# Attention output as values by transposed weights, with the softmax division moved to GpSimd ahead of it

## The chip, the cores and the metric

The kernel runs on one core of one Trainium2 chip. The metric is the device time of one execution in microseconds. Three runs of the kernel before took 2192.15, 2194.88 and 2196.93 us, so its median is 2194.88 us.

## The reference

The program is a trunk of two layers (`DEPTH = 2`) over 512 tokens of width 1024. Each layer is a SwiGLU half-step, a mixer with three groups of heads, and a second SwiGLU half-step. The change touches two of the three groups:

```
# group A: 6 heads x 64, each of 4 blocks of 128 queries, keys 0 .. end of the block,
#          128 keys chosen per query by an indexer, bias by distance
logits = q @ k.T / 8 + bias (+ -inf for keys not chosen or not admissible)
p      = softmax(logits, axis=-1)
out_a  = p @ v                       # 128 queries x 64, per head
# group C: 4 heads x 64, every query over 256 memory tokens
p      = softmax(q @ k_mem.T / 8, axis=-1)
out_c  = p @ v_mem
x      = x + concat(out_a, out_b, out_c) @ w_out
```

A softmax is exp(logit - maximum) divided by the row's sum. The division can be done on the weights (128 x keys) or on the output (128 x 64), with the same result but for rounding.

## The kernel before

**Engines and queues.** Each engine runs its own program in order. The order of work in the mixer is written out by hand in one list, `MIX_ORDER` (L197 to L363), which every engine walks through, doing its own share of each step and waiting on semaphores for the others. All large products are done in three passes over rounded halves (XH, XL of the activations, wh, wl of the weights; lines 886, 887, 888, the helper `three`). Weights come in units of 1 MB: SP loads `raw`, ScalarE (or, for units 16 and 17 of the mixer, GpSimd in `round_weights`, L851) makes `wh`, VectorE makes `wl` (`split_lo_rows`, L1724).

**Attention.** A job is one head for one block of 128 queries. Two jobs with neighbouring heads form a pair, and 20 pairs make a layer's attention: pairs 0 to 7 are memory jobs (256 keys), 8 to 10 are block 0 of group A (128 keys), 11 to 13 block 1 (256 keys), 14 to 16 block 2 (384), 17 to 19 block 3 (512). They go through a pipeline of 24 slots, `("att", slot)` in `MIX_ORDER`. In slot s the engines do:

- TensorE, in this order (`attention`, L1265): if a phase (a block of one group) ended with pair s-4, transposes of the divided output `oA` (L1271); transposes of the weights `at` of pair s-2 (L1285), after `je_done`; the logits of pair s (L1301), two heads in the two row halves of the array; the output of pair s-3 (L1317), with the transposed weights `pT` (128 x 128) as the stationary operand and the values (128 x 64) as the moving one, one 128 x 64 output per head in bank 3.
- VectorE (`attention`, L1988): the low half `XL` of a finished phase (L1995); the reciprocals `rrec` of all sums of a phase at its end (L2003); the row maxima of pair s (L2022 with bias, L2026 without); at the end of a phase the output times the reciprocals into `oA` (L2033).
- ScalarE (L1602): exp of pair s-1 with the row sum (L1616); the high half `XH` of a finished phase (L1623); copies of the transposed weights of pair s-2 from PSUM to `pT` (L1634).
- GpSimd (`combine`, L832): the sum of bias strip and mask for pair s+2, from pair 11 on, so in slots 9 to 17 (L848).

**What fills the gaps.** Between the slots `MIX_ORDER` puts rounds of the output projection on TensorE (`out_round`, L1035, one round is the three instructions of lines 886 to 888 with 512 columns): 3, 3, 2, 3, 3, 2, 3, 3, 2, 2 of them after slots 3 to 12, then 1, 1, 1, 2, 1, 1, 1, 2, 1, 1 after slots 13 to 22. On VectorE there are a selection round in slots 5 to 12 (L1830, L1832), the additions of finished rounds into `xT` (L2063) and pieces of `wl` (L1734). After slot 22 the rest of the projection follows in one piece (`TAIL`).

Of the kernel before, what the change touches and what calls it, by code (L numbers as in the profile page):

```python
# [14 lines left out]
P = 128  # L15
# [492 lines left out]
jl_done jm_done je_done jtr_done jp_even jp_odd jv_done  # L508
o_ev o_t o_hi o_lo
# [3 lines left out]
def hybrid_trunk(nc, xt, memt, cols, strip_table, weights, consts, out):  # L513
    depth = cols.shape[1]

    with ExitStack() as ctx:
# [119 lines left out]
        oA = sb("oA", [P, WA])  # L636
# [41 lines left out]
        with nc.Block() as block:  # L678
# [56 lines left out]
            def _(pool):  # L735
                def layer(L):
# [94 lines left out]

                    def combine(p):  # L832

                        for n in (2 * p, 2 * p + 1):
                            if n >= N_JOBS:
                                return
                            b, j = job(n)
                            if b and j < H_A:
                                m = masked_count(b, j)
                                w = P * (b + 1)  # L840
                                if m == 1:
                                    pool.wait_ge(S["strip_in"], 48)
                                    pool.wait_ge(S["jv_done"], M_JOBS)
                                if j == 0:
                                    pool.wait_ge(S["unsel_done"], b)
                                if m > 4:
                                    pool.wait_ge(S["jm_done"], n - 3)
                                pool.tensor_tensor(comb[(m - 1) % 4][:, 0:w], strips[j][:, T - w:], unsel[b][:, :],  # L848
                                                   ALU.add).then_inc(S["cb_done"], 1)
# [8 lines left out]
                    for step in MIX_ORDER:  # L858
                        if step[0] == "att":
                            combine(step[1] + 2)  # L860
# [13 lines left out]
            def _(pe):  # L874
                def layer(L):
# [389 lines left out]
                    def attention(slot):  # L1265
                        p = slot - 4
                        if 0 <= p < N_PAIRS and phase_end(p):
                            b, ph, done = phase(2 * p)
                            pe.wait_ge(S["o_ev"], done + 1)
                            for c in range(3 if ph else 2):  # L1270
                                mm = pe.transpose(bank[3][:, c * P:(c + 1) * P], oA[:, c * P:(c + 1) * P],  # L1271
                                                  const("ident"))
                            mm.then_inc(S["o_t"], 1)
                        p = slot - 2
                        if 0 <= p < N_PAIRS:
                            for e in range(2):
# [4 lines left out]
                                pe.wait_ge(S["je_done"], n + 1)  # L1281
# [22 lines left out]
                        if 0 <= p < N_PAIRS:  # L1304
                            for e in range(2):
                                n = 2 * p + e
                                b, j = job(n)
                                pe.wait_ge(S["jp_odd" if e else "jp_even"], p + 1)
                                if n == 0:
                                    pe.wait_ge(S["os_read"], of("os_read", NB))  # L1310
                                if j in (0, H_A) and n:
                                    pe.wait_ge(S["o_lo"], phase(n)[2])
                                nt = b + 1 if j < H_A else 2
                                at0 = DH * (j if j < H_A else j - H_A)
                                for i in range(nt):
                                    v = (dvN[:, i, at0:at0 + DH] if j < H_A else mvN[:, i, at0:at0 + DH])
                                    mm = pe.matmul(bank[3][:, at0:at0 + DH], pT[n % 4][:, i * P:(i + 1) * P], v,  # L1317
                                                   start=(i == 0), stop=(i == nt - 1))
                                mm.then_inc(S["jv_done"], 1)
# [30 lines left out]
            def _(act):  # L1350
# [21 lines left out]
                def layer(L):  # L1372
# [229 lines left out]
                    def attention(slot):  # L1602
# [16 lines left out]
                        if 0 <= p < N_PAIRS and phase_end(p):  # L1619
                            b, ph, done = phase(2 * p)  # L1620
                            act.wait_ge(S["o_t"], done + 1)
# [60 lines left out]
            def _(dve):  # L1682
# [27 lines left out]
                def layer(L):  # L1710
# [277 lines left out]
                    def attention(slot):  # L1988
# [8 lines left out]
                        p = slot - 3  # L1997
                        ends = 0 <= p < N_PAIRS and phase_end(p)
                        if ends:
                            b, ph, done = phase(2 * p)  # L2000
                            j0, nh = (0, H_A) if ph else (H_A, H_M)
                            dve.wait_ge(S["je_done"], 2 * p + 2)
                            chain.step(dve.reciprocal(rrec[:, b % 2, j0:j0 + nh], rsum[:, b % 2, j0:j0 + nh]))  # L2003
                            chain.join()
# [22 lines left out]
                        if ends:  # L2027
                            p = slot - 3
                            b, ph, done = phase(2 * p)
                            j0, nh = (0, H_A) if ph else (H_A, H_M)  # L2030
                            dve.wait_ge(S["jv_done"], 2 * p + 2)
                            r = rrec[:, b % 2, j0:j0 + nh].unsqueeze(2).to_broadcast([P, nh, DH])
                            dve.tensor_tensor(oA[:, 0:nh * DH].rearrange("p (h d) -> p h d", h=nh),  # L2033
                                              bank[3][:, 0:nh * DH].rearrange("p (h d) -> p h d", h=nh), r,
                                              ALU.mult).then_inc(S["o_ev"], 1)
# [135 lines left out]
```

## Time and profile before

| | us |
|---|---|
| median of 3 runs | 2194.88 |
| lowest and highest run | 2192.15, 2196.93 |
| span of the profiled execution, first to last instruction | 2192.3 |
| TensorE busy | 2169.3 (99%) |
| VectorE busy | 1076.5 (49%) |
| ScalarE busy | 765.7 (35%) |
| GpSimd busy | 383.4 (17%) |

The span is what the profile shows of the execution's own time; the profile states no other time for it, and the three timed runs lie from 0.2 us below to 4.6 us above it. A fp32 product or a fp32 weight load stands in the trace as two records, a transpose or a rounded (fp32r) product as one. In the timelines the first column is the start in us from the start of the span, the second the length of the merged piece; the ends of TensorE's records are modelled, so what an instruction costs TensorE is read here from its start to the start of the next.

### The profile page before, as it was taken

The page shows a single profiled execution, that of the slowest core. Times are in us where ns is not written, and L with a number is a line of the kernel's source. Part 1 is how long each engine was busy: PE and PEld are TensorE (multiplying, and loading weights), DVE is VectorE, ACT ScalarE, POOL GpSimd, SP SyncE. Part 2 cuts the span into 40 slices and gives each one's busy share as a digit, 9 for nine tenths or more (in the row PEclk, how much of TensorE's full clock was granted, in tenths as well). Part 3 has the DMA queues.
Part 4 walks back from the last instruction along what each step waited for, and adds up shares of the span by engine and source line. Part 5 has one row for each costly group of instructions (what it writes and reads, how often), then busy time and mean ns, then how long its engine had stood idle before and what let it go on. Part 6 is the DMA issues. An engine that isn't in the chain of part 4 may idle for free.

```text
span 2192.3 us, 32889 instructions
## 1 busy us (share of the span) xinstructions
PE 2169.3 (99%) x13657; PEld 1755.9 (80%) x13657; DVE 1076.5 (49%) x1473; ACT 765.7 (35%) x1038; POOL 383.4 (17%) x319
## 2 busy tenths in 40 slices
PE   9999999999999999999999999999999999999999
PEld 7888888777777888888888888887777778888887
DVE  5333333788657544333343433338877666333322
ACT  5222223474335332222232222234733454222211
POOL 0111012005223410101111110130151134111000
PEclk9999999999999999999999999999999999999999
DMA  5222233221011222223222222232211112322232
GB/s 190 96 96 96 89 105 114 97 97 31 32 68 39 78 96 96 96 91 106 93 96 97 96 100 99 89 125 86 97 41 39 51 39 80 112 96 96 91 105 73
DMA packets 30649, 192.40 MB, mean 88 GB/s; under 512 B 3216, under 2 KB 5392, under 8 KB 11984
## 3 DMA queue, kind: packets, MB, share of 16 engines
q1 hardware_dynamic: 30160, 189.80, 25.4%
q8 instruction: 81, 1.33, 0.2%
q10 hardware_dynamic: 384, 1.07, 0.1%
q14 instruction: 24, 0.20, 0.0%
HBM read 188.64 MB, written 2.10 MB: 87 GB/s over the span
## 4 chain that ended last, share of the span: by engine, by line
PE 91%; DVE 5%; ACT 2%; issue 1%; DMA 0%; SPq 0%; DVEq 0%; ACTq 0%
PE psum L886 27%; PE psum L888 26%; PE psum L887 26%; PE psum L1317 2%; PE psum L1169 1%; PE psum L1017 1%; PE psum L1301 1%; PE psum L1189 1%; PE psum L1285 1%; DVE acc L1817 1%; PE psum L1259 1%; PE psum L1227 1%; DVE XL L1749 1%; PE psum L1221 1%; DVE wl L1734 1%
## 5 line engine op out<-in xcount | busy, mean ns | idle before, releaser
L886 PE MATMUL psum<-XH,wh 128*128 128x512 f32 x1904 | 763.4, 401 | 4.9 <-DVE wl L1734 1.8
L888 PE MATMUL psum<-XH,wl 128*128 128x512 f32 x1904 | 743.8, 391 | 0.0
L887 PE MATMUL psum<-XL,wh 128*128 128x512 f32 x1904 | 743.7, 391 | 0.0
L886 PEld LDWEIGHTS psum<-XH,wh 128*128 128x128 f32 x1904 | 358.6, 188 | 93.2 <-issue 14.6
L888 PEld LDWEIGHTS psum<-XH,wl 128*128 128x128 f32 x1904 | 358.6, 188 | 76.0
L887 PEld LDWEIGHTS psum<-XL,wh 128*128 128x128 f32 x1904 | 358.8, 188 | 74.1 <-issue 4.3
L1742 DVE TENSOR_TENSOR wl<-raw,wh 128x2048 fp32r<-128x2048 f32 x88 | 201.7, 2292 | 159.4 <-ACT wh L1387 159.4
L886 PE MATMUL psum<-HH,wh 128*128 128x512 f32 x704 | 273.9, 389 | 0.0
L887 PE MATMUL psum<-HL,wh 128*128 128x512 f32 x704 | 273.9, 389 | 0.0
L888 PE MATMUL psum<-HH,wl 128*128 128x512 f32 x704 | 273.9, 389 | 0.0
L1382 ACT ACTIVATE wh<-raw 128x2048 fp32r<-128x2048 f32 (+1 forms) x84 | 157.2, 1872 | 307.6 <-PE psum L888 307.4
L750 POOL TENSOR_TENSOR sg<-sg,rF 128x512 f32<-128x512 f32 x88 | 113.5, 1292 | 783.5 <-ACT sg L1412 783.5
L1720 DVE TENSOR_TENSOR wl<-raw,wh 128x2048 fp32r<-128x2048 f32 x52 | 122.1, 2347 | 251.4 <-ACT wh L1382 251.3
L1387 ACT ACTIVATE wh<-raw 128x2048 fp32r<-128x2048 f32 x88 | 167.4, 1902 | 13.1 <-PE psum L888 13.1
L1418 ACT ACTIVATE HH<-hf 128x512 f32 (+1 forms) x88 | 55.6, 632 | 328.3 <-DVE hf L1771 328.3
L1412 ACT ACTIVATE sg<-sg 128x512 f32<-128x512 f32 x88 | 55.2, 631 | 292.9 <-DVE sg L1763 292.9
L1763 DVE TENSOR_TENSOR sg<-psum,rF 128x512 f32<-128x512 f32 x88 | 60.1, 687 | 193.5 <-PE psum L888 172.2
L886 PEld LDWEIGHTS psum<-HH,wh 128*128 128x128 f32 x704 | 132.1, 188 | 27.6
L887 PEld LDWEIGHTS psum<-HL,wh 128*128 128x128 f32 x704 | 132.1, 188 | 27.6
L888 PEld LDWEIGHTS psum<-HH,wl 128*128 128x128 f32 x704 | 132.1, 188 | 27.1
L1771 DVE TENSOR_TENSOR hf<-sg,psum 128x512 f32<-128x512 f32 x88 | 60.4, 687 | 134.2 <-PE psum L888 125.8
L672 POOL TENSOR_TENSOR sg<-xT 128x512 f32<-128x512 f32 x40 | 47.8, 1196 | 395.9 <-DVE xT L1786 333.4
(255 smaller groups left out, 2123.1 us busy)
## 6 DMA issues: line engine op xcount, KB each, us to landing
raw<-weights SPq DMA_DIRECT2D x143, 1024.0 KB, 4.9
raw<-weights SPq DMA_DIRECT2D x32, 896.0 KB, 4.6
xT<-xt SPq DMA_DIRECT2D x4, 512.0 KB, 6.4
memT<-memt SPq DMA_DIRECT2D x2, 1024.0 KB, 4.7
out<-xT SPq DMA_DIRECT2D x8, 256.0 KB, 5.6
stripsA<-strip_table SPq DMA_DIRECT2D x2, 768.0 KB, 6.7
raw<-weights SPq DMA_DIRECT2D x2, 512.0 KB, 6.6
stripsB<-strip_table SPq DMA_DIRECT2D x2, 512.0 KB, 7.3
```

Of the source, the lines that this page charges most:

```text
L750: pool.tensor_tensor(sg[fs][:, :], sg[fs][:, :], rF[:, :], ALU.mult).then_inc(S["gr_done"], 1)
L886: pe.matmul(out_ap, a_hi, b_hi, start=first, stop=False)
L887: pe.matmul(out_ap, a_hi, b_lo, start=False, stop=False)
L888: return pe.matmul(out_ap, a_lo, b_hi, start=False, stop=last)
L1382: ins = act.activation(wh[u % 2][:, k0:k1, :], raw[u % 2][:, k0:k1, :], ACT.Copy)
L1387: act.activation(wh[j][:, :, :], raw[j][:, :, :], ACT.Copy).then_inc(S["w_hi"], 1)
L1412: act.activation(sg[fs][:, :], sg[fs][:, :], ACT.Silu).then_inc(S["gs_done"], 1)
L1418: act.activation(HH[:, 2 * i + fs, :], hf[fs][:, :], ACT.Copy).then_inc(S["hh_done"], 1)
L1720: dve.tensor_tensor(wl[u % 2][:, :, :], raw[u % 2][:, :, :], wh[u % 2][:, :, :].bitcast(F32), ALU.subtract).then_inc(S["w_lo"], 1)
L1742: dve.tensor_tensor(wl[j][:, :, :], raw[j][:, :, :], wh[j][:, :, :].bitcast(F32), ALU.subtract).then_inc(S["w_lo"], 1)
L1763: dve.tensor_tensor(sg[fs][:, :], bank[fs][:, :], rF[:, :], ALU.mult).then_inc(S["g_free"], 1)
L1771: dve.tensor_tensor(hf[fs][:, :], sg[fs][:, :], bank[2 + fs][:, :], ALU.mult).then_inc(S["u_free"], 1)
```

## The change

The two heads of a pair now put their values (128 x 64) in as stationary operands, one in each column half of the array, and the transposed weights (128 queries wide) stream through. The output comes out as 2 x 64 rows by 128 queries, which is the form that the projection wants, so `oA`, its multiplication and the transposes of it go. The division by the sum can then no longer be applied to the output's partitions, so it is done on the weights before they are transposed: VectorE takes the reciprocals pair by pair, in slot s for pair s-1 after the maxima of pair s, and GpSimd multiplies each job's weights by them in `normalise`, in slot s for pair s-1 ahead of `combine`. TensorE's transposes wait for that (`jn_done`) instead of for the exp.

```diff
+                    def normalise(p):
+                        if 0 <= p < N_PAIRS:
+                            pool.wait_ge(S["jr_done"], p + 1)
+                            for n in (2 * p, 2 * p + 1):
+                                b, j = job(n)
+                                w = P * (b + 1) if j < H_A else NM
+                                pool.tensor_scalar(at[n % 4][:, 0:w], at[n % 4][:, 0:w], rrec[:, b % 2, j:j + 1], None,
+                                                   ALU.mult).then_inc(S["jn_done"], 1)
...
                         if step[0] == "att":
+                            normalise(step[1] - 1)
                             combine(step[1] + 2)
...  TensorE, attention(slot)
-                            pe.wait_ge(S["o_ev"], done + 1)
-                            for c in range(3 if ph else 2):
-                                mm = pe.transpose(bank[3][:, c * P:(c + 1) * P], oA[:, c * P:(c + 1) * P],
-                                                  const("ident"))
-                            mm.then_inc(S["o_t"], 1)
...
-                                pe.wait_ge(S["je_done"], n + 1)
+                                pe.wait_ge(S["jn_done"], n + 1)
...
-                                for i in range(nt):
-                                    v = (dvN[:, i, at0:at0 + DH] if j < H_A else mvN[:, i, at0:at0 + DH])
-                                    mm = pe.matmul(bank[3][:, at0:at0 + DH], pT[n % 4][:, i * P:(i + 1) * P], v,
+                            for i in range(nt):
+                                for e, r in enumerate(rows):
+                                    mm = pe.matmul(bank[3][r, at0:at0 + P],
+                                                   vals[:, i, at0 + DH * e:at0 + DH * (e + 1)],
+                                                   pT[(2 * p + e) % 4][:, i * P:(i + 1) * P],
                                                    start=(i == 0), stop=(i == nt - 1))
...  ScalarE
-                            act.wait_ge(S["o_t"], done + 1)
+                            act.wait_ge(S["jv_done"], 2 * p + 2)
...  VectorE, attention(slot)
-                            dve.wait_ge(S["je_done"], 2 * p + 2)
-                            chain.step(dve.reciprocal(rrec[:, b % 2, j0:j0 + nh], rsum[:, b % 2, j0:j0 + nh]))
-                            chain.join()
...
-                            dve.tensor_tensor(oA[:, 0:nh * DH].rearrange("p (h d) -> p h d", h=nh),
-                                              bank[3][:, 0:nh * DH].rearrange("p (h d) -> p h d", h=nh), r,
-                                              ALU.mult).then_inc(S["o_ev"], 1)
+                        p = slot - 1
+                        if 0 <= p < N_PAIRS:
+                            b, j = job(2 * p)
+                            dve.wait_ge(S["je_done"], 2 * p + 2)
+                            dve.reciprocal(rrec[:, b % 2, j:j + 2], rsum[:, b % 2, j:j + 2]).then_inc(S["jr_done"], 1)
```

## Rows read from the trace of the kernel before

**Rows 1.** The page: the chain that ended last, share of the span by engine.
```profile
PE 91%; DVE 5%; ACT 2%; issue 1%; DMA 0%; SPq 0%; DVEq 0%; ACTq 0%
```
**Rows 2.** Table by windows, first layer: PE, PEld, DVE, ACT, POOL; clock, DMA.
```profile
638.00:641.00 3.00, 1.44 (x10) 0.70 (x8) 2.11 (x4) 3.00 (x12) 3.00 (x4) 0.93 0.00 0
641.00:644.00 3.00, 2.91 (x13) 2.26 (x13) 3.00 (x5) 1.53 (x6) 0.53 (x1) 0.50 0.00 0
```
**Rows 3.** Timeline of TensorE, first layer: slots 5, 12, 16 to 17, 19, start of TAIL.
```profile
653.87 0.70 PE L1301 MATMUL psum<-mkT,mqT 64*128 64x256 f32 x4
...
681.06 0.70 PE L1301 MATMUL psum<-dkT,dqT 64*128 64x256 f32 x4
...
694.17 0.92 PE L1301 MATMUL psum<-dkT,dqT 64*128 64x384 f32 x4
695.01 1.10 PE L1317 MATMUL psum<-dvN,pT 128*128 128x64 f32 x8
695.93 0.48 PE L886 MATMUL psum<-XH,wh 128*128 128x512 f32 x1
...
697.72 0.82 PE L1285 MATMUL psum<-cst,at 128*128 128x128 f32 x6
698.47 1.13 PE L1301 MATMUL psum<-dkT,dqT 64*128 64x512 f32 x4
...
706.59 1.13 PE L1301 MATMUL psum<-dkT,dqT 64*128 64x512 f32 x4
...
722.66 0.46 PE L886 MATMUL psum<-XH,wh 128*128 128x512 f32 x1
```
**Rows 4.** Groups by line: the output products and the transposes that go.
```profile
L1317 PE MATMUL psum<-dvN,pT 128*128 128x64 f32 x240 | 31.3, 277 | 1.3 <-DVE XL L1995 1.1
...
L1317 PE MATMUL psum<-mvN,pT 128*128 128x64 f32 x128 | 18.9, 294 | 0.8 <-DVE XL L1995 0.8
...
L1271 PE MATMUL psum<-cst,oA 128*128 128x128 f32 x40 | 7.3, 281 | 1.2 <-DVE oA L2033 1.2
```
**Rows 5.** TensorE's idle time at line 1271, by what ended it: us, times.
```profile
  DVE oA L2033: 4.7, 8
```
**Rows 6.** Timeline of TensorE in the recurrence: one column half; both in turn; one tile.
```profile
588.72 0.56 PE L1235 MATMUL psum<-U,kdc 64*64 64x64 f32 x12
589.12 0.52 PE L1241 MATMUL psum<-AT,U 64*64 64x64 f32 x12
589.47 0.86 PE L1259 MATMUL psum<-gvN,XTF 64*64 64x64 f32 x12
...
593.43 0.87 PE L1221 MATMUL psum<-Sbd,WT 128*64 128x128 f32 x6
594.23 0.88 PE L1227 MATMUL psum<-EGr,Sbd 128*128 128x64 f32 x6
```
**Rows 7.** GpSimd by line and shape: busy us, mean ns of one.
```profile
L855 POOL CAST wh<-raw 128x1024 fp32r<-128x1024 f32 x8 | 8.9, 1156 | 6.7 <-PE psum L888 6.7
L848 POOL TENSOR_TENSOR comb<-stripsA,acc 128x512 f32<-128x512 f32 x6 | 7.6, 1290 | 4.1 <-DVE mxs L2022 4.1
...
L848 POOL TENSOR_TENSOR comb<-stripsA,acc 128x256 f32<-128x256 f32 x6 | 4.3, 740 | 66.8 <-issue 66.8
```
**Rows 8.** Timeline of VectorE: slots 5 to 6 and 18.
```profile
654.60 0.76 DVE L2026 TENSOR_REDUCE mxs<-psum 128x1 f32<-128x256 f32 x2 [0.22 <-PE psum L1301]
655.27 0.68 DVE L1830 MAX8 m<-wrk 128x8 f32<-128x512 f32 x1
...
656.66 0.68 DVE L2063 TENSOR_TENSOR xT<-psum,xT 128x512 f32<-128x512 f32 x1
657.25 0.17 DVE L2003 RECIPROCAL rrec<-rsum 128x4 f32<-128x4 f32 x1
...
703.59 0.69 DVE L2022 CUSTOM_DVE_ANT_0 at<-psum,comb 128x512 f32<-128x512 f32 x1 [2.64 <-PE psum L1301]
...
704.81 1.22 DVE L1734 TENSOR_TENSOR wl<-raw,wh 128x1024 fp32r<-128x1024 f32 x1
```

More of the change, by code:

```diff
@@ L507 @@
 v_t v_done gc_ps gc_ready row_ps row_ready
-jl_done jm_done je_done jtr_done jp_even jp_odd jv_done
-o_ev o_t o_hi o_lo
+jl_done jm_done je_done jr_done jn_done jtr_done jp_even jp_odd jv_done
+o_hi o_lo
 """.split()
@@ L1265, in attention @@
                     def attention(slot):
-                        p = slot - 4
-                        if 0 <= p < N_PAIRS and phase_end(p):
-                            b, ph, done = phase(2 * p)
-                            pe.wait_ge(S["o_ev"], done + 1)
-                            for c in range(3 if ph else 2):
-                                mm = pe.transpose(bank[3][:, c * P:(c + 1) * P], oA[:, c * P:(c + 1) * P],
-                                                  const("ident"))
-                            mm.then_inc(S["o_t"], 1)
                         p = slot - 2
@@ L1304, in attention @@
                         if 0 <= p < N_PAIRS:
[L1305 to L1314, printed above, removed]
-                                for i in range(nt):
-                                    v = (dvN[:, i, at0:at0 + DH] if j < H_A else mvN[:, i, at0:at0 + DH])
-                                    mm = pe.matmul(bank[3][:, at0:at0 + DH], pT[n % 4][:, i * P:(i + 1) * P], v,
+                            b, j = job(2 * p)
+                            pe.wait_ge(S["jp_even"], p + 1)
+                            pe.wait_ge(S["jp_odd"], p + 1)
+                            if p == 0:
+                                pe.wait_ge(S["os_read"], of("os_read", NB))
+                            elif j in (0, H_A):
+                                pe.wait_ge(S["o_lo"], phase(2 * p)[2])
+                            nt = b + 1 if j < H_A else 2
+                            vals, at0 = (dvN, DH * j) if j < H_A else (mvN, DH * (j - H_A))
+                            for i in range(nt):
[3 more added lines that the diff above has]
+                                                   pT[(2 * p + e) % 4][:, i * P:(i + 1) * P],
                                                    start=(i == 0), stop=(i == nt - 1))
-                                mm.then_inc(S["jv_done"], 1)
+                                    if i == nt - 1:
+                                        mm.then_inc(S["jv_done"], 1)
                     if L == 0:
@@ L1996, in attention @@
                                               XH[sl].bitcast(F32), ALU.subtract).then_inc(S["o_lo"], 1)
[L1997 to L2001, printed above, removed]
-                            dve.wait_ge(S["je_done"], 2 * p + 2)
-                            chain.step(dve.reciprocal(rrec[:, b % 2, j0:j0 + nh], rsum[:, b % 2, j0:j0 + nh]))
-                            chain.join()
                         p = slot
@@ L2026, in attention @@
                                     dve.tensor_reduce(m, src, AX.X, ALU.max, negate=True).then_inc(S["jm_done"], 1)
[L2027 to L2032, printed above, removed]
-                            dve.tensor_tensor(oA[:, 0:nh * DH].rearrange("p (h d) -> p h d", h=nh),
-                                              bank[3][:, 0:nh * DH].rearrange("p (h d) -> p h d", h=nh), r,
-                                              ALU.mult).then_inc(S["o_ev"], 1)
+                        p = slot - 1
+                        if 0 <= p < N_PAIRS:
+                            b, j = job(2 * p)
+                            dve.wait_ge(S["je_done"], 2 * p + 2)
+                            dve.reciprocal(rrec[:, b % 2, j:j + 2], rsum[:, b % 2, j:j + 2]).then_inc(S["jr_done"], 1)
                     ffn(0)
```

1 line of the change is left out of this document (removed).

## The prediction

> **What bounds the kernel now.** I read the chain of waits first. TensorE carries 91% of it [rows 1], and the table in the section above has it busy for 2169.3 of 2192.3 us, so a TensorE instruction that goes pays its full time, as long as TensorE does not then meet a wait. All of the change lies in the attention stage, which in the first layer runs from about 632 to 722.66 us and again in the second. There the timeline of TensorE shows the slots as a fixed sequence [rows 3]: transposes, logits, output products, rounds. The logits of slots 5, 12 and 19 start at 653.87, 681.06 and 706.59, with lengths on TensorE of 0.64, 0.64 and 1.06 (L in the list below), so they end at 654.5, 681.7 and 707.65: 27.2 us for seven slots, then 25.9 us for seven. Those three ends and 722.66 are my marks. The table by windows is the third view: the one low-clock stretch of the stage, 0.50 at 641 to 644, comes right after three microseconds in which TensorE was busy for 1.44 [rows 2].
>
> The pieces of a slot, read from start to next start [rows 3, 8]:
> - T, the transposes of a pair at 384 keys: 697.72 to 698.47, 0.75; by six transposes against two, four and eight, 0.31, 0.53 and 0.97 for 128, 256 and 512 keys.
> - L, the logits at 384 keys: 694.17 to 695.01, 0.84, and by 0.21 less or more for each 128 keys: 0.42, 0.64, 1.06.
> - R, a round: 695.93 to 697.72 holds two and three of the transposes that go (0.11 each): 0.73, and I use 0.70.
> - M, both maxima of a pair: 654.60 to 655.27, 0.67 at 256 keys; 703.59 to 704.81, 1.22 at 512; 0.95 between, 0.42 at 128. A reciprocal is 0.17; a selection round 655.27 to 656.66, 1.4; an addition into xT 0.6; a half of `wl` 1.1 to 1.2.
> - A wait passed from one engine to the next costs about 0.1: the step from the end of the logits to the maxima is 0.1.
>
> **The change part by part.**
>
> *Output products.* Before, 368 records are busy for 31.3 + 18.9 = 50.2 us [rows 4]; from start to next start eight of them (a pair at 256 keys) take 695.01 to 695.93, 0.92 [rows 3], so 0.46 per 128 keys of a pair, 0.115 a record. After, there are as many records, each a load of 64 columns and a stream of 128. The nearest row is L1221, the very form, six records in one column half: 593.43 to 594.23, 0.133 each [rows 6]. If the two halves of the array work one after the other, this is the price and 0.07 per 128 keys is lost (upper bound, 0.53). Whether they work at once, the neighbouring rows tell: L1235 feeds the column halves in turn and starts 12 records in 0.40 us, 0.033 each; L1259 has all 12 in one tile and lasts 0.86, 0.07 each. So halves in turn run twice as fast. I take half of 0.133, which is also twice L1235's 0.033 for a stream twice as wide: V = 0.27, 0.53, 0.80, 1.07 us for 128, 256, 384, 512 keys, against 0.46, 0.92, 1.38, 1.84. The lower bound is L1235's 0.033 itself, half of that.
>
> The trace shows a gap ahead of narrow tiles (it is inside the 0.133). The Trainium skill (TensorEngine Tiling (Array Packing), Key Properties) says that changing the tiling mode drains TensorE, which speaks against this change: each pair gets one switch more, from the row halves of the logits to column halves and on to the whole array. By the page the switch would be paid whole instead of half, an estimate of 0.1 us more a pair, so some 2 us more where TensorE is the bound; the sum goes by the rows.
>
> *The end of a phase.* 40 transposes go (L1271, 0.11 each, 4.4 us), and with them TensorE's wait for `oA`, 4.7 us in 8 places [rows 5]. VectorE loses 16 multiplications and gets 24 reciprocals more, about even.
>
> *The new link.* For pair q-1 the weights are now ready only after: logits of q end, 0.1, M(q), reciprocal 0.17, 0.1, two normalisations 2N, 0.1. Then come T(q-1) and L(q+1), and only then the next link can begin. Behind the waiting transposes on TensorE stand those logits, and behind them all of the slot; behind the reciprocal on VectorE stand selection, additions and `wl`; behind `normalise` on GpSimd stand `combine` and, in slots 1 to 4, the casts of units 16 and 17. What covers the link on TensorE is V(q-3) and the rounds, from 0.27 + 1.4 to 0.53 + 2.1 early, but only V + 0.7 from slot 13 on.
>
> *N.* No row shows GpSimd with one tensor input and a column of scalars. Bounds: the cast, 1024 elements in 1.156 us, which is 1.1 ns an element with one input; the sum of two tensors, 0.74, 1.0, 1.29 for 256, 384, 512 [rows 7]. The rows of sums make 2.15 ns an element and 0.19 fixed; with this fixed part in the cast, 0.86 to 0.95 an element are left. I take N = 0.29, 0.40, 0.51, 0.62 us for 128, 256, 384, 512 keys, since the operation has one tensor input as the cast has. The lower end is the cast without a fixed part, 0.14 to 0.58, the upper the row of sums.
>
> The skill (GPSIMD Engine Reference, Elementwise — side-by-side cycle accounting) gives 769 ns measured for 512 elements of a tight one-input loop. The cast here is faster than that. With an estimate of N = 0.77 at 512 from that page the total below would be some 3 us higher.
>
> *Slots 0 to 5.* Slot 2 is held at 637.7 by the copy of the last values as before. Transposes of pair 1 wait for maxima that VectorE takes at 638.8, a reciprocal and 0.8 of GpSimd, until 640.6; the logits behind them begin at about 641.2 instead of 641.09. The casts of units 16 and 17 move from 637 to 641.5 apart, to 637.6, 640.6, 645 and 650; VectorE asks for them at 640.6, 644, 649 and after 660, so only their order changes. In slots 3 and 4 the shorter V brings about 1, and `oA` no longer stands before `wl` of unit 17, for which TensorE waits near 651: 0.5. Logits of slot 5 end at 653.0 instead of 654.5: -1.5.
>
> *Slots 5 to 12.* Period = max(V + R, link) + T + L, with VectorE not later than its own work. Slot 5: V + R 1.93, link 0.1 + 0.67 + 0.17 + 0.1 + 0.8 + 0.1 = 1.94, with T and L 3.12 (before 3.54). The same sum gives for slots 6 to 11: 3.80, 3.58, 3.05, 3.38, 3.70, 2.72, where VectorE is late by 0.5 in slot 8, and in slot 10 `combine` of pair 11, which waits for the last memory outputs, keeps normalise 0.1 too long. Sum 23.35 against 27.2: -3.85.
>
> *Slots 12 to 19.* Slot 12 has the last selection round (2.7 us) on VectorE, so maxima 13 start 0.5 late. Periods by the link: 3.30, 3.9, 3.63, 4.07, 4.28, 4.54, 4.98 = 28.7 against 25.9: +2.75. An example, slot 16: 0.1 + 0.95 + 0.17 + 0.1 + 1.02 + 0.1 + 0.75 + 1.06 = 4.25. TensorE alone would need 0.53 + 1.4 + 0.75 + 1.06 = 3.7 there, 2.8 in slot 15, 3.5 in slot 18: it now waits 0.5 to 1.5 a slot. GpSimd has 2N + 2.55 of `combine` = 3.6 in the fullest slot and is not the bound.
>
> *Slots 20 on.* T of pair 18 waits until 2.95 after the last logits (1.5 of it covered), then T 0.97, V 1.07, two rounds 1.4, T 0.97, V 1.07, R 0.7, V 1.07, R 0.7, and the two last rounds 1.4 cover the copies of the output: 12.3 against 15.01: -2.7.
>
> Sum: -1.5 - 3.85 + 2.75 - 2.7 = -5.3 a layer, -10.6 in both. On the profiled execution 2192.3 - 10.6 = 2181.7. The span is 2.6 below the median of the runs shown; with what lies around it unchanged, 2194.9 - 10.6 = 2184.3.
>
> **The rivals.**
>
> *GpSimd is slow: slower than before.* One mechanism: N at the rate of the two-tensor row. For: it is the only arithmetic of GpSimd in the trace. Against: the cast. Each link from slot 12 on gets 0.68, 0.68, 0.98 three times, 1.34, 1.35 longer, 7.0 a layer; the slots with two rounds lose 0.7 three or four times, 2.5; slots 0 to 4 0.5. +20 in all: 2204. It turns to slower where the sum of both normalisations of a 512 pair passes about 2.0 us.
>
> *The gain is eaten.* N midway (0.95 at 512), or the column halves taking turns: V then is 0.53 per 128 keys; the early slots and the end of the stage give back 6.5 to 7 a layer, the late ones nothing, since the link covers it. 2193 to 2198. For: the one row of this form shows no gain. Against: L1235.
>
> *The clock.* Waiting 15 to 40% of each late slot, TensorE falls to its lower level (0.50 is 1.2 GHz), as it did after 638 to 641. T, L, V and R double in seven slots and become the bound at 5 to 7.5 us each: about 14 a layer, 2212. Against: there it was busy less than half of three us, here 60 to 85%.
>
> *It doesn't do what it says*, the products staying as long, is in the second rival. *Better than forecast*: N without fixed part (0.1 to 0.3 a link from slot 12 on, 1.5 a layer) and V half as long (0.27 in eight pairs early and at the end, 2): 2177.
>
> **How the numbers follow.** About 0.2% (4.4 us) is what a measurement of this kernel can tell from no change. The forecast 0.50, with 2184.3 as its time and 2179 to 2190 as its range, better 0.08; the gain eaten 0.20; GpSimd slow 0.15; the clock 0.05; the rest, 0.02, with the slow ones. Faster: 0.50 + 0.08 and a little of the eaten cases, 0.60; same 0.19; slower 0.21. The range leaves out the clock and the worst of GpSimd: 2176 to 2203.
>
> **What would show it.** In the new profile: the output products start at 0.065 to 0.07 a record (0.13 would be the turn-taking halves); `tensor_scalar` on GpSimd at 0.6 for 512 keys (1.3 is the slow rival); TensorE idle before its transposes with GpSimd's normalise as releaser, some 9 us a layer, nearly all after slot 12; logits of slot 5, 12 and 19 earlier by 1.5, 5.4 and 2.6 us than before in the first layer; no low clock but near 641. The prediction is wrong if the waits before the transposes are also there in slots 5 to 11, or if VectorE's reciprocal comes late because it waits behind selection or `wl`.

## The result and the profile after

The changed kernel took 2219.78 us (median of 4 runs, 2216.25 to 2223.03) against 2194.51 us (2192.15 to 2196.93) for the kernel before on the same chip: a ratio of 1.0116, 95% interval 1.0102 to 1.0131. It is 25 us slower; the prediction said 10.6 us faster, and the time lies outside its range. The profiled execution has a span of 2220.5 us (before: 2192.3). TensorE has less work than before, but is busy for 2172.5 us, 3.2 more, and idle for 48.0 us instead of 23.0: part of the loss is waiting, and part stands inside records that became longer at a low clock.

The new multiplications by shape, with the output products and the transposes, whole run (columns as in [rows 4]: busy us, mean ns of one, idle time before and its releaser):

```profile
L838 POOL TENSOR_SCALAR at<-at,rrec 128x256 f32<-128x256 f32 x44 | 51.2, 1175 | 31.9 <-DVE rrec L2027 31.9
L1287 PE MATMUL psum<-cst,at 128*128 128x128 f32 x184 | 38.0, 311 | 35.4 <-POOL at L838 35.2
L1318 PE MATMUL psum<-pT,dvN 128*64 128x128 f32 x240 | 22.0, 323 | 0.0
L838 POOL TENSOR_SCALAR at<-at,rrec 128x512 f32<-128x512 f32 x12 | 20.4, 1711 | 10.9 <-DVE rrec L2027 10.9
L838 POOL TENSOR_SCALAR at<-at,rrec 128x384 f32<-128x384 f32 x12 | 14.8, 1243 | 4.2 <-DVE rrec L2027 4.2
L1318 PE MATMUL psum<-pT,mvN 128*64 128x128 f32 x128 | 11.4, 304 | 0.0
L838 POOL TENSOR_SCALAR at<-at,rrec 128x128 f32<-128x128 f32 x12 | 7.1, 603 | 4.5 <-PE psum L1318 3.3 <-DVE rrec L2027 1.3
```

The reader is to see three things. The products are shorter: 22.0 + 11.4 = 33.4 us of records against 31.3 + 18.9 [rows 4]. TensorE idles 35.4 us ahead of the transposes of the weights, 35.2 of them for line 838 (18.8 us in 24 waits in the first layer, where the prediction had some 9 a layer), and its weight loads wait longer still (52.2 us in the whole run). And one multiplication of 512 keys takes 1.71 us, beyond even the 1.29 of the sum of two tensors [rows 7].

The timeline of TensorE, first layer, at the prediction's four marks (columns as in [rows 3]; in brackets the idle time ahead and its releaser):

```profile
655.37 0.70 PE L1303 MATMUL psum<-mkT,mqT 64*128 64x256 f32 x4
656.00 0.66 PE L1318 MATMUL psum<-pT,mvN 128*64 128x128 f32 x8
656.59 0.50 PE L896 MATMUL psum<-XH,wh 128*128 128x512 f32 x1
...
682.31 0.70 PE L1303 MATMUL psum<-dkT,dqT 64*128 64x256 f32 x4
682.94 0.44 PE L1318 MATMUL psum<-pT,dvN 128*64 128x128 f32 x4
...
707.01 0.88 PE L1318 MATMUL psum<-pT,dvN 128*64 128x128 f32 x12
707.82 0.50 PE L896 MATMUL psum<-XH,wh 128*128 128x512 f32 x1
...
716.75 1.11 PE L1287 MATMUL psum<-cst,at 128*128 128x128 f32 x4 [2.32 <-POOL at L838]
718.28 1.11 PE L1287 MATMUL psum<-cst,at 128*128 128x128 f32 x4 [0.43 <-POOL at L838]
719.33 2.08 PE L1303 MATMUL psum<-dkT,dqT 64*128 64x512 f32 x4
721.34 1.55 PE L1318 MATMUL psum<-pT,dvN 128*64 128x128 f32 x12
...
730.15 1.09 PE L1318 MATMUL psum<-pT,dvN 128*64 128x128 f32 x16
731.18 0.50 PE L896 MATMUL psum<-XH,wh 128*128 128x512 f32 x1
...
735.30 0.40 PE L896 MATMUL psum<-XH,wh 128*128 128x512 f32 x1
```

The logits of slots 5, 12 and 19 end at 656.0, 682.9 and 721.3 (before: 654.5, 681.7, 707.65), and the tail starts at 735.3 (722.66). From mark to mark, in us of one layer:

| stretch | before | forecast | after | after minus forecast |
|---|---|---|---|---|
| to the end of slot 5's logits | 654.5 | 653.0 | 656.0 | +3.0 |
| slots 5 to 12 | 27.2 | 23.35 | 26.9 | +3.6 |
| slots 12 to 19 | 25.95 | 28.7 | 38.4 | +9.7 |
| slot 19 to the tail | 15.0 | 12.3 | 14.0 | +1.7 |

The last column sums to 18.0 us: the first layer is 12.6 us slower than before where the sum had it 5.3 faster (rounding aside). The span grew by 28.2 us, which leaves 15.6 for the second layer, so it went the same way and lost 3 us more. Twice 18.0 and these 3 are the whole error of 38.8 us in the span (2181.7 forecast, 2220.5 measured).

Now GpSimd and VectorE beside each other, five links of the first layer (two timelines, GpSimd first):

```profile
640.83 3.23 POOL L838 TENSOR_SCALAR at<-at,rrec 128x256 f32<-128x256 f32 x2 [1.16 <-DVE rrec L2027]
...
660.92 1.83 POOL L838 TENSOR_SCALAR at<-at,rrec 128x256 f32<-128x256 f32 x2 [2.08 <-DVE rrec L2027]
664.85 2.72 POOL L838 TENSOR_SCALAR at<-at,rrec 128x256 f32<-128x256 f32 x2 [2.10 <-DVE rrec L2027]
...
714.24 3.99 POOL L838 TENSOR_SCALAR at<-at,rrec 128x512 f32<-128x512 f32 x2 [0.71 <-DVE rrec L2027]
722.92 3.10 POOL L838 TENSOR_SCALAR at<-at,rrec 128x512 f32<-128x512 f32 x2 [4.69 <-DVE rrec L2027]
```
```profile
640.65 0.67 DVE L1989 TENSOR_TENSOR XL<-gzT,XH 128x512 fp32r<-128x512 f32 x1
641.24 1.22 DVE L1738 TENSOR_TENSOR wl<-raw,wh 128x1024 fp32r<-128x1024 f32 x1
...
660.75 0.67 DVE L1834 MAX8 m<-wrk 128x8 f32<-128x512 f32 x1
...
662.12 0.68 DVE L2055 TENSOR_TENSOR xT<-psum,xT 128x512 f32<-128x512 f32 x1
...
664.68 1.20 DVE L1738 TENSOR_TENSOR wl<-raw,wh 128x1024 fp32r<-128x1024 f32 x1
...
714.06 1.20 DVE L1738 TENSOR_TENSOR wl<-raw,wh 128x1024 fp32r<-128x1024 f32 x1
```

The pair at 660.92, beside selection and an addition that reads PSUM, takes 1.83, 0.92 a head. The pair at 664.85, beside 1.2 us of `wl`, takes 2.72: 0.9 more. With `wl` and XL beside it, at 640.83, 1.4 more; at 714.24, 0.9 more than the pair at 722.92. `wl` itself stays at 1.2 us, so it is GpSimd that gives way, and the 0.9 us are about what was left of `wl` when GpSimd started (664.85, with `wl` running from 664.68 to the next start at 665.80). It is no chance meeting: the reciprocal releases GpSimd, and the piece of `wl` stands right behind the reciprocal in VectorE's list. In the Trainium skill, the table in GPSIMD Engine Reference, Specifications, says that GpSimd shares its SBUF interfaces with VectorE and contends with instructions of two SBUF inputs; the trace agrees, `wl` and XL having two and the addition at 662.12 one.

The table by windows (PE, PEld, DVE, ACT, POOL; clock, DMA): three windows of the late slots of the first layer, and from the same view one that holds those of the second:

```profile
700.00:715.00 15.00, 11.27 (x71) 6.14 (x71) 6.50 (x19) 8.28 (x20) 13.37 (x12) 1.00 0.00 0
715.00:719.00 4.00, 1.83 (x8) 1.42 (x8) 0.86 (x2) 0.60 (x2) 3.23 (x2) 0.72 0.63 207
719.00:723.00 4.00, 4.00 (x19) 1.84 (x18) 1.39 (x5) 1.43 (x4) 0.08 (x1) 0.50 0.13 55
...
1776.00:1813.00 37.00, 31.43 (x160) 17.43 (x158) 19.78 (x61) 18.21 (x53) 29.60 (x31) 0.86 0.00 1
```

Behind the wait of 2.32 us the granted clock is 0.50, which is 1.2 GHz, for the transposes, the logits and the output products of slot 19. The second transposes and the logits stand in the chain: 1.05 and 2.01 us from start to next start instead of 0.58 (726.08 to 726.66) and 1.06, so 1.4 us. The products take 1.47 instead of 0.81, but the next transposes wait for GpSimd behind them in any case. (A low stretch after slot 2 is in both kernels: 0.56 from 640 to 645 before, 0.65 from 645 to 650 after.) In the second layer the clock falls more often: 0.86 in the mean over 37 us, where the same slots of the first layer stood at 1.00 up to 715. The logits of slot 15 in both layers:

```profile
695.63 0.92 PE L1303 MATMUL psum<-dkT,dqT 64*128 64x384 f32 x4
...
1798.53 1.65 PE L1303 MATMUL psum<-dkT,dqT 64*128 64x384 f32 x4
...
1840.41 0.40 PE L896 MATMUL psum<-XH,wh 128*128 128x512 f32 x1
```

The last line is the start of the second tail. From the end of slot 12's logits to the tail the second layer takes 55.8 us (1784.62 to 1840.41), the first 52.4 (682.94 to 735.30), while in the kernel before this stretch has the same length in both layers (41.0). GpSimd's multiplications in it are as long in both layers to 0.01 us a pair. So these 3.4 us are the low clock, and but for 0.4 that come back elsewhere they are the 3 us that the second layer lost more. The clock fell there behind a wait of 1.73 us, ahead of the transposes at 1791.61. The same wait is in the first layer (1.74 ahead of 689.95), where the clock stayed at 2.4 GHz; why, no run shows.

### The profile page after: what moved, and what is told of

It reads as the page before. It is cut to its first block and busy times, and to the rows that moved or that the text cites. A ratio compares the mean times of both kernels' runs of the same rounds, so it can differ in the third digit from the quotient of the medians.

```text
span 2220.5 us, 32911 instructions
## 1 busy us (share of the span) xinstructions
PE 2172.5 (98%) x13617; PEld 1734.2 (78%) x13617; DVE 1068.7 (48%) x1481; ACT 769.0 (35%) x1038; POOL 473.3 (21%) x399
## 3 DMA queue, kind: packets, MB, share of 16 engines
q10 hardware_dynamic: 384, 1.07, 0.1%
## 5 line engine op out<-in xcount | busy, mean ns | idle before, releaser
L897 PEld LDWEIGHTS psum<-HL,wh 128*128 128x128 f32 x704 | 132.2, 188 | 27.2
```

The lines of the kernel that those rows point to most:

```text
L897: pe.matmul(out_ap, a_hi, b_lo, start=False, stop=False)
```

## The experiments

Each edit is against the changed kernel, but for the one that says otherwise. Each was timed beside the kernel before, and the ratio is to that; the medians of the kernel before beside them were 2194.7, 2192.2 and 2195.4 us, so a difference of under 3 us between two experiments means nothing by itself.

**No division: the change without its link.** GpSimd's multiplication is left out and the transposes wait for the exponential, so the weights stay undivided.

```diff
-                            normalise(step[1] - 1)
...
-                                pe.wait_ge(S["jn_done"], n + 1)
+                                pe.wait_ge(S["je_done"], n + 1)
```

> The changed kernel without the division of the weights (GpSimd's normalise left out, the output stays undivided; transposes wait for the exp as before). Theory (the new link through GpSimd is the loss, the output products themselves gain): 2170 to 2182 us, the output products at 0.59 us a pair of 256 keys from start to start, no idle time of TensorE ahead of its transposes, clock at its upper level as before. Rival (the products in column halves, with one more change of tiling a pair, are the loss): 2200 us or more, since they are unchanged here.

Measured: 2170.56 us, ratio 0.9898 (0.988 to 0.9916). As expected, at the lower edge. The logits of slots 12 and 19 start at:

```profile
675.41 0.70 PE L1302 MATMUL psum<-dkT,dqT 64*128 64x256 f32 x4
...
698.46 1.13 PE L1302 MATMUL psum<-dkT,dqT 64*128 64x512 f32 x4
```

Slots 12 to 19 take 23.5 us (from 676.04 to 699.52, the ends of the logits) instead of 38.4. The products and the end of the phases are worth 24 us; the link costs 49.

**The link alone, on the kernel before.** The old products, `oA` and its transposes stay, with `normalise`, its reciprocals and the new wait added, so the output is divided twice.

```diff
+                            normalise(step[1] - 1)
...
-                                pe.wait_ge(S["je_done"], n + 1)
+                                pe.wait_ge(S["jn_done"], n + 1)
```

> The kernel before with the link alone: reciprocals pair by pair behind the maxima, weights multiplied on GpSimd, transposes of the weights wait for it. The output products stay in the old form, the output is multiplied by the reciprocals again and transposed as before (so the division is done twice, which makes the output another one). Theory (the link costs more than the rest of the change gains, above all in slots 12 to 19, where it sets the period whatever the products take): slots 12 to 19 at 36 to 39 us as in the change, 2222 to 2238 us. Rival (link and products only lose together, for instance by the changes of tiling): 2200 to 2210 us.

Measured: 2232.02 us, ratio 1.0172 (1.0143 to 1.0201), and slots 12 to 19 in 36.7 us. As expected. Alone the link costs 37.5 us (39.8 against the kernel before timed beside it, 2192.2), with the shorter products 49: these no longer cover it. From here the products bring back only 12 to 15 us (2232.0 to 2219.8, or by the two differences to the kernel before) of the 24 that they are worth without it.

**VectorE multiplies, behind the reciprocal.**

```diff
-                            normalise(step[1] - 1)
...  VectorE, behind the reciprocal of the pair
+                                dve.tensor_scalar(at[n % 4][:, 0:w], at[n % 4][:, 0:w], rrec[:, b % 2, j:j + 1], None,
+                                                  ALU.mult).then_inc(S["jn_done"], 1)
```

> The changed kernel with the same multiplication of the weights on VectorE, right behind its reciprocal, instead of on GpSimd. Theory (GpSimd's slow tensor_scalar is the price, 0.92 to 1.7 us each; a VectorE tensor_scalar over 512 elements took 0.43 us in the selection): link shorter by 1.3 to 2.5 us a slot, 2180 to 2192 us. Rival A (any division ahead of the transposes costs about this, since the wait for the maxima of the next pair is what matters): 2205 us or more. Rival B (VectorE becomes the bound in slots 5 to 12, where selection runs): faster than the change, but slots 5 to 12 longer than before the change.

Measured: 2201.49 us, ratio 1.0035 (1.0023 to 1.0046). A miss, by 10 us. The timeline of VectorE shows the same line 2031 at very different lengths, with GpSimd's `combine` beside the second and third (the second fence):

```profile
643.62 0.62 DVE L2031 TENSOR_SCALAR at<-at,rrec 128x256 f32<-128x256 f32 x2
...
692.09 1.66 DVE L2031 TENSOR_SCALAR at<-at,rrec 128x256 f32<-128x256 f32 x2
...
696.76 2.38 DVE L2031 TENSOR_SCALAR at<-at,rrec 128x384 f32<-128x384 f32 x2
```
```profile
692.54 1.06 POOL L857 TENSOR_TENSOR comb<-stripsC,acc 128x384 f32<-128x384 f32 x1
...
696.31 2.62 POOL L857 TENSOR_TENSOR comb<-stripsA,acc 128x512 f32<-128x512 f32 x2 [2.72 <-DVE mxs L2017]
```

Alone it needs 0.31 a head at 256 keys, beside `combine` 0.83, and the pair of 384 ends only when `combine` does. Here it is VectorE that gives way, and I had left that out. In both kinds of meeting the instruction that started second is the one that became longer: `wl` had started ahead of GpSimd's multiplication above, `combine` (691.58, 696.31) ahead of VectorE's here. The short multiplication saves 18 us of the changed kernel's time; that this stretching is what keeps it from more is argued from these lines, no run takes it away. The rival in which VectorE's selection becomes the bound is out: slots 5 to 12 take 25.95 us here (653.87 to 679.82), less than the 26.9 of the change and the 27.2 of before.

**The reciprocal ahead of the maxima.** The five lines of the reciprocal move from behind the maxima of pair s to the front of slot s in VectorE's list; GpSimd multiplies as in the change.

```diff
+                            dve.reciprocal(rrec[:, b % 2, j:j + 2], rsum[:, b % 2, j:j + 2]).then_inc(S["jr_done"], 1)
                             (row maxima of pair s)
-                            dve.reciprocal(rrec[:, b % 2, j:j + 2], rsum[:, b % 2, j:j + 2]).then_inc(S["jr_done"], 1)
```

> The changed kernel with VectorE's reciprocal of pair s-1 ahead of the maxima of pair s instead of behind them; GpSimd multiplies as in the change. Theory (the loss is a loop logits, maxima, reciprocal, GpSimd, transposes, next logits inside one slot; its place in the order matters as much as GpSimd's speed): the multiplication no longer stands behind the maxima of the next pair, what is left is GpSimd's own load of about 5 us in slots 15 to 17: 2180 to 2195 us. Rival (only the time of GpSimd's instructions matters, and it meets other work anyway): within 8 us of the change, 2212 to 2222.

Measured: 2194.12 us, ratio 0.9996 (0.9986 to 1.0005): as expected, at the upper edge. The logits of q and their maxima leave the link, and 25.7 us come back; the time is that of before. The rival, that only the time of GpSimd's instructions matters, is out.

**Two-tensor form.** The multiplication on GpSimd as `tensor_tensor`, the column of reciprocals spread over the keys.

```diff
-  pool.tensor_scalar(at[n % 4][:, 0:w], at[n % 4][:, 0:w], rrec[:, b % 2, j:j + 1], None,
+  pool.tensor_tensor(at[n % 4][:, 0:w], at[n % 4][:, 0:w],
+                     rrec[:, b % 2, j:j + 1].to_broadcast([P, w]),
```

> The changed kernel with GpSimd's tensor_scalar written as tensor_tensor with the reciprocal's column broadcast along the keys. Theory (the instruction's time is the term that was mis-sized): 0.74, 1.0 and 1.29 us for 256, 384 and 512 keys as the two-tensor rows have it, against 0.92, 1.24 and 1.55 alone, so 0.4 to 0.5 us less a slot, 2204 to 2213 us. Rival (GpSimd's time is not what the slots wait for): same as the change within 3 us.

Measured: 2199.34 us, ratio 1.0028 (1.0018 to 1.0037). A miss, 5 us better than I expected:

```profile
L838 POOL TENSOR_TENSOR at<-at,rrec 128x512 f32<-128x512 f32 x12 | 13.9, 1190 | 7.9 <-DVE rrec L2028 7.9
L838 POOL TENSOR_TENSOR at<-at,rrec 128x384 f32<-128x384 f32 x12 | 9.7, 827 | 4.0 <-DVE rrec L2028 4.0
```

The form with two tensors is the quicker one at every width (0.83 against 1.24 us at 384), and quicker than the sum of two tensors, which takes 1.0 there, between the two of [rows 7]. Same place, same waits, same engine: 20.4 us from the size of N alone.

**The same instruction over half the keys.** GpSimd multiplies the first half of each job's keys; the other half stays undivided.

```diff
-  pool.tensor_scalar(at[n % 4][:, 0:w], at[n % 4][:, 0:w], rrec[:, b % 2, j:j + 1], None,
+  pool.tensor_scalar(at[n % 4][:, 0:w // 2], at[n % 4][:, 0:w // 2], rrec[:, b % 2, j:j + 1], None,
```

> The changed kernel, but GpSimd multiplies only the first half of the keys of each job; the weights of the other half go to the transposes undivided (so they are not softmax weights). Order, waits and instruction counts stay; only the width of the multiplication is halved. My theory (the size of this multiplication was the term that the prediction had wrong; 0.60, 0.93, 1.24 and 1.55 us for 128, 256, 384 and 512 keys when alone in the changed kernel): the multiplication falls by about half, to 0.3, 0.6, 0.76 and 0.92 us alone, close to but still above the 0.29, 0.40, 0.51 and 0.62 us that the prediction took. So 2188 to 2200 us, slots 12 to 19 in 26 to 32 us instead of 38.4. Rival (the place in the order and the wait, not the width, cost the time): 2212 us or more.

Measured: 2199.13 us, ratio 1.0018 (1.0009 to 1.0028); slots 12 to 19 take 711.38 + 1.06 - 679.72 = 32.7. By the median as expected at its edge, by the slots just above it: N means 0.77 for the 192 columns of a 384 pair. The fixed part does not halve:

```profile
L838 POOL TENSOR_SCALAR at<-at,rrec 128x192 f32<-128x192 f32 x6 | 4.5, 766 | 2.1 <-DVE rrec L2027 2.1
L838 POOL TENSOR_SCALAR at<-at,rrec 128x64 f32<-128x64 f32 x6 | 2.6, 447 | 2.5 <-PE psum L1318 1.8 <-DVE rrec L2027 0.6
```

With 0.60, 0.92, 1.24 and 1.55 for 128 to 512 columns that makes one line, 0.29 us fixed and 2.45 ns a column.

**ScalarE multiplies**, as an activation (Copy) with the reciprocals as its scale, last in its share of the slot. Once with the reciprocal ahead of the maxima, and once behind them as in the change.

```diff
-                            normalise(step[1] - 1)
...  ScalarE, end of attention(slot)
+                            act.wait_ge(S["jr_done"], p + 1)
+                            for n in (2 * p, 2 * p + 1):
+                                act.activation(at[n % 4][:, 0:w], at[n % 4][:, 0:w], ACT.Copy,
+                                               scale=rrec[:, b % 2, j:j + 1]).then_inc(S["jn_done"], 1)
```

> The changed kernel with the reciprocal ahead of the maxima and the weights multiplied on ScalarE (Copy with the reciprocal's column as scale) at the end of its slot. Theory (what cost the time is the pair of GpSimd and VectorE getting in each other's way and the loop behind the maxima; ScalarE is busy for half of a slot and is not stretched by either): 0.45 to 0.7 us an instruction, slots 13 to 18 at most 4.1 us each (ScalarE's own sum at 512 keys: exp 1.8, copies 1.1, multiplications 1.3), 2174 to 2184 us. Rival (ScalarE, with 4 us of work in the late slots, becomes the bound and its copies to pT come late): slots 12 to 19 above 30 us, 2190 us or more.

> The multiplication on ScalarE (2174.6 us when the reciprocal stands ahead of the maxima), with the reciprocal back behind the maxima as in the changed kernel: the fourth cell of place against engine (GpSimd behind 2219.8, ahead 2194.1). Theory (the place sets when the factor is there, some 0.5 us later per slot, and ScalarE's queue then holds the exponentials of the next slot back behind the wait): 2182 to 2196 us. Rival (only the engine counts): 2172 to 2178 us.

Measured: 2174.56 us ahead (2172.95 to 2177.41, ratio 0.9915, 0.9886 to 0.9943), and 2195.97 us behind (ratio 1.001, 0.9998 to 1.0021). Both as expected, at the lower and at the upper edge. The first beats both kernels, 17.7 us below the kernel before timed beside it (2192.22) and some 4 us above the kernel with no division. Its group at 256 keys, and TensorE's wait for it in the attention stage of the first layer (us, times, longest):

```profile
L1645 ACT ACTIVATE at<-at,rrec 128x256 f32<-128x256 f32 x44 | 20.0, 506 | 4.5 <-DVE rrec L2012 4.5
```
```profile
PE psum L1286 <- ACT at L1645: 0.8, 1, 0.8
```

That is 0.8 us where the same view of the changed kernel has 18.8. Its weight loads of that line wait some more for ScalarE (4.5 us in the whole run).

**Both mends of GpSimd's link together**: reciprocal ahead, two-tensor form.

> The two edits that each gave about 20 to 25 us together: the reciprocal ahead of the maxima on VectorE, and the multiplication on GpSimd as a two-tensor operation with the reciprocals' column spread over the keys. Theory (place and size of the link both count, and what is left once the link is short is GpSimd's own load): 2183 to 2190 us. Rival (GpSimd's load alone bounds it in either form): 2192 us or more. If both gains simply add: 2174 us.

Measured: 2177.95 us (2177.85 to 2182.88), ratio 0.992 (0.9904 to 0.9937). A miss on the good side. The two gains, 25.7 and 20.4, nearly add: 41.8 of 46.1 us. I had supposed GpSimd's load to be the next bound. TensorE's waits for it in the first layer, weight loads and products:

```profile
PEld psum L1287 <- POOL at L838: 6.7, 12, 1.4
...
PE psum L1287 <- POOL at L838: 3.1, 6, 1.2
```

The cells side by side, in us:

| who multiplies | reciprocal behind the maxima | ahead of them |
|---|---|---|
| GpSimd, one tensor and a column | 2219.8 (the change) | 2194.1 |
| GpSimd, two tensors | 2199.3 | 2178.0 |
| ScalarE | 2196.0 | 2174.6 |

The place is worth 21 to 26 us in each row. Going from one tensor and a column on GpSimd to either other operation is worth 20 to 24 us with the reciprocal behind and 16 to 20 with it ahead. ScalarE's multiplication is longer than VectorE's is alone (0.31), but nothing stretches it: its mean at 256 keys is 0.50 and 0.51 in the two kernels, where GpSimd's is 1.01 and 1.18.

**One head after the other.** The output products with the loops swapped: all of head 1, then all of head 2, so that the column halves do not alternate.

```diff
-                            for i in range(nt):
-                                for e, r in enumerate(rows):
+                            for e, r in enumerate(rows):
+                                for i in range(nt):
```

> The changed kernel with the output products of a pair in another order: all blocks of keys of the first head (one column half of the array), then all of the second. Same instructions, same waits. Theory (the gain of the products comes from the two column halves working at once when fed in turn): a pair of 256 keys takes about 1.0 us from start to start instead of 0.59, one of 512 about 1.8 instead of 1.03; where the link covers it nothing is lost, so some 3 to 6 us a layer: 2225 to 2231 us. Rival (the products are short because 128 columns stream per load, whatever the order): 0.59 stays and the time is that of the change within 3 us.

Measured: 2222.94 us, ratio 1.0131 (1.01 to 1.0161), whose interval overlaps the change's (1.0102 to 1.0131). A miss: neither the expected loss nor the expected length of the pair of 256 keys came. Timeline of TensorE, a pair of 256, 384 and 512 keys with the round behind it:

```profile
698.72 0.67 PE L1318 MATMUL psum<-pT,dvN 128*64 128x128 f32 x8
699.31 0.50 PE L896 MATMUL psum<-XH,wh 128*128 128x512 f32 x1
...
714.89 1.15 PE L1318 MATMUL psum<-pT,dvN 128*64 128x128 f32 x12
715.97 0.50 PE L896 MATMUL psum<-XH,wh 128*128 128x512 f32 x1
...
728.92 1.58 PE L1318 MATMUL psum<-pT,dvN 128*64 128x128 f32 x16
730.43 0.50 PE L896 MATMUL psum<-XH,wh 128*128 128x512 f32 x1
```

1.08 against 0.81 us at 384 keys and 1.51 against 1.03 at 512: fed in turn, the halves do run beside each other. But the pair of 256 keys takes 0.59 either way, which I had not expected and cannot explain from the rows. In time it matters little; that the link covers most of the products would explain it, but is argued here, not measured.

## Why the prediction was wrong, step by step

**Output products (V): right.** Forecast 0.27, 0.53, 0.80, 1.07; measured 0.37 (682.94 to 683.31, four records), 0.59, 0.81, 1.03. Only the narrow pairs are off, by 0.06 to 0.1, as a fixed 0.16 a pair would make it: 0.16 + 0.215 per 128 keys fits all four. The rival in which the halves take turns, 0.53 per 128 keys, is out. The switch of tiling that the prediction left outside its sum, at 0.1 us a pair, fits the narrow pairs and not the pair of 512; no run takes the switch apart from the rest.

**End of a phase: right in kind.** The wait for `oA` and the 40 transposes are gone; the kernel with no division gets 12 us a layer from this and V. The prediction read the wait for `oA` too large: of its 4.7 us only 1.2 is idle time of the products' records [rows 4], the rest is that of the weight loads ahead of the same transposes.

**N: the step that failed.** "I take N = 0.29, 0.40, 0.51, 0.62 us for 128, 256, 384, 512 keys, since the operation has one tensor input as the cast has." It measured 0.60, 0.92, 1.24, 1.55 alone and 0.60, 1.18, 1.24, 1.71 in the mean: alone 2.1 to 2.5 times the value, and above the upper bound of 0.74, 1.0, 1.29 as well. The estimate of 0.77 at 512 keys that stood beside the sum was half of the measured 1.55. The reason given was wrong: the count of tensor inputs does not order GpSimd's operations. The cast of 1024 columns takes 1.03 to 1.16 us, this multiplication of 512 takes 1.55 with one tensor and 1.04 in the mean with two (the kernel with both mends).

In the forecast's own sum that explains most of what the first layer lost. Slots 12 to 19 hold seven pairs of multiplications, measured in the trace at 1.82, 2.78, 1.82, 2.46, 2.46, 2.46 and 3.99 where 2N was 0.8 three times, 1.02 three times and 1.24: 11.1 us more, and the stretch came out 9.7 later, with 1.4 us of low clock in it. The four pairs of slots 1 to 4 have 7.8 more, of which V and the rounds cover all but 3.0; the seven of the next stretch 6.8 more, of which 3.6 came through; the pair at 722.92 has 1.9 more, and the end came out 1.7 later.

**The link's form and its price: about right.** With N at 0.74 to 1.29 the sum gave 2204; the two-tensor kernel, whose N is 0.60 to 1.19, took 2199.3, and halving the width took the time to 2199.1. Both have meetings with `wl` and stretches of low clock (mean clock 0.993) that the sum had not, so part of the agreement is luck. No kernel here has a link on GpSimd as short as the forecast's. Halving the width took 0.6, 0.9 and 1.3 us off the pairs of 256, 384 and 512 keys and gave 20.6 us; the forecast's N is 0.4, 0.5 and 0.6 a pair below that again, and by proportion my estimate is some 2186 to 2189 us, inside the forecast's range. "It turns to slower where the sum of both normalisations of a 512 pair passes about 2.0 us": at 2.4 us (two-tensor) it was 1.0028 of before, at 3.4 us 1.0116.

**Contention: left out.** A pair of multiplications that meets `wl` is 0.9 us longer. In the first layer that struck five of the twenty pairs (640.83, 646.91, 652.23, 688.00, 714.24) hard on the path and one (664.85) in the covered slots; it is the 1.18 in place of 0.92.

**The clock: half right.** I gave this rival 0.05 and priced it for seven slots. In the first layer it came in one more than before, slot 19, behind the window in which TensorE was busy 1.83 of 4 us: 1.4 us in the chain. The slots before, busy 11.27 of 15 us, kept 2.4 GHz. In the second layer it came in more of them, and this layer lost 3.4 us to it beyond the first. So some 6 us in all where the rival had 28. It goes with the waits: with ScalarE multiplying, the span's mean clock is 0.996 as before (the changed kernel's 0.989).

**Engine order: as forecast.** The prediction named a reciprocal stuck behind selection or `wl` as what would make it wrong; it starts 0.8 us after the logits end (660.67 behind 659.90), as in the sum. Waits ahead of the transposes do appear before slot 12, which the text gave as its other sign of being wrong. What I did not ask is whether it had to stand behind the maxima at all: the sums it needs are those of the pair before, and moving it gains 21 to 26 us.

What stays open: why the clock fell in the second layer and not in the first behind the same waits, why a pair of 256 keys does not mind the order of the halves, and how the 24 us of gain without the link divide between V and the end of a phase.

## What to carry to other kernels

On GpSimd the rows of neighbouring operations did not bound one that the trace of before does not show: it took 2.1 to 2.5 times what the cast suggested and 1.2 times the row of sums. Before trusting a gain of half a per cent, ask what the sum gives with such a term doubled, or put the operation on an engine whose rate a row shows. When work is moved into a chain between two engines, look for the earliest point at which each input exists, and at which instruction stands next on the neighbouring engine. And a shorter product on the bound engine is worth only what the chain beside it leaves uncovered: 24 us here without the link, 12 to 15 with it.

## What the runs showed of the hardware

- GpSimd, fp32, one tensor times a column: 0.29 us + 2.45 ns a column (0.45 at 64 to 1.55 at 512). The same product with the column as a second tensor: 0.38, 0.60, 0.81 for 128, 256, 384. The Trainium skill (GPSIMD Engine Reference, Elementwise — side-by-side cycle accounting) puts `tensor_tensor` with its two inputs at about 2.6 cycles an element and the best case of a tight loop at 1.8. With the 1.2 GHz of that section, the 2.15 ns of the sums in [rows 7] are an estimated 2.6 cycles, which agrees; one tensor times a column is an estimated 2.9, slower than two full tensors.
- Sharing goes both ways. A pair of GpSimd's multiplications is 0.9 us longer where it starts just behind VectorE's `wl` of 1.2 us (two SBUF inputs) and unchanged beside selection or additions from PSUM; VectorE's multiplication grows from 0.31 to 0.83 us beside GpSimd's sum that had started before it, while `wl` beside GpSimd stays at 1.2. The selection's multiplication of 512 columns on VectorE (`acc`) takes 0.43 us with GpSimd idle (before) and 1.11 behind a `combine` that started 0.25 us ahead of it (after, 686.04).
- ScalarE's Copy with a scale column: 0.40, 0.51, 0.61, 0.72 us for 128, 256, 384 and 512 columns, with the reciprocal ahead or behind, and pairs of one width alike to 0.02 us through the first layer.
- Two column halves in alternation: 0.215 us per 128 x 128 block of a pair; one after the other 1.08 and 1.51 us for three and four blocks.
